# Two transformer blocks on one core: which attention of the first block runs first, and how its steps are spaced

## The chip, the cores and the metric

The kernel runs on one core of a Trainium2 chip. The metric is the device time in microseconds (us) from launch to end, the median of a few executions. TensorE (PE) multiplies matrices, VectorE (DVE) and ScalarE (ACT) work elementwise on SBUF and PSUM, GpSimd (POOL) elementwise on SBUF alone, SyncE (SP) issues transfers.

## The reference

Two transformer blocks follow each other on one sequence of 512 tokens, width 1024, fp32. The change concerns the order of work in the first block, and one spacing that both blocks share. Cut to what matters:

```
def first_block(x, ...):
    proj = rms_norm(x, norm1_g) @ w_in
    qa, ka, va, qb, kb, vb, gate_a, gate_b = split(proj)
    out_a = chunked_attention(qa, ka, va, q_gain, k_gain, rel_bias)  # head norms, bias, softmax
    out_b = stick_breaking_attention(qb, kb, vb)                     # sigmoid, reversed cumulative product
    mixed = sigmoid(gate_a) * (out_a @ w_branch_a) + sigmoid(gate_b) * (out_b @ w_branch_b)
    x = x + mixed @ w_out
    return x + conv_glu(rms_norm(x, norm2_g), ...)

def second_block(x, ...):
    ...  # hgrn2 mixer, and forgetting_attention (head norms, decay, causal softmax)
    merged = gate_h * (y_h @ w_branch_a) + gate_f * (y_f @ w_branch_b)
    ...  # then out projection, gated FFN, and a last gated projection
```

out_a and out_b don't depend on each other.

## The kernel before

Every weight matrix is streamed once, in **slots** of 128 x 512 numbers (256 KB). SP loads a slot into one of four raw buffers; ACT rounds it to a high half `w_hi` (L841), GpSimd subtracts to get the low half `w_lo` (L642); PE does twelve matmuls of 512 columns with it, three products for each of four 128-wide tiles (L1514). The halves have eight buffers, so conversions run up to seven slots ahead of PE.

One list, `SCHEDULE`, gives the order of all work; each engine walks it and does its own part of each entry, strictly in that order, waiting on semaphores for the others. `run(names, plan)` writes the slots of the phases in `names`, numbered from 0 across them; an entry of `plan` with number n stands behind slot n. A phase of one group has eight slots (`branch` phases have two groups of four, `gate` phases two of eight). Behind the last slot of a group stands a `take`: its four PSUM tiles are read out, by ACT or DVE as `OWNER` says (a = ACT, d = DVE), then a `fill` (the conversion of a later slot), and then the plan's entries of that number. PE starts the next group in the same banks, tile by tile as each is taken. In the first block the numbers are: qA 0 to 7, kA 8 to 15, vA 16 to 23, qB 24 to 31, kB 32 to 39, vB 40 to 47, gateA 48 to 63, branchA 64 to 71, gateB 72 to 87, and branchB in a list of its own. In the second: hi, hg, fq, fk, fv 0 to 39, gateH 40 to 55, branchH 56 to 63, gateF 64 to 79.

An attention (A and B in the first block, F in the second) is 16 steps, one per pair of heads and block of 128 queries, and three more to drain; step i handles (i mod 4 + 1) x 128 keys. On PE (`att_pe`) a step does its scores into banks 4 and 5 (L1438), at steps 6, 10, 14 and 18 the product with v for a finished pair (L1453), and the transposes of the probabilities of step i - 2 (L1465). Between lie chains on other engines:

- A: DVE adds the bias and finds the maximum (L1106), ACT takes exp (L757), DVE the reciprocal (L1138), ACT scales (L773); a finished pair is copied by ACT (L766) and its low half formed by DVE (L1144).
- F: as A, with three DVE instructions for bias and maximum (L1116 to L1120), and part of the transposed probabilities copied by ACT (L760).
- B: DVE masks (L1100), ACT takes two sigmoids per head (L748, L749), DVE scans (L1133), GpSimd multiplies (L694).

Head norms (`square`, `scale`) of q and k come ahead of A and F: ACT squares, PE averages (L1612), ACT takes Ln and Exp (L956, L958), DVE scales.

ACT keeps one table of functions; `uses(name)` loads another where the next entry needs it (L848). Exp and Ln are in one, sigmoid is in another, copies work with any. The takes of gateA, gateB, gateH and gateF are sigmoids (L926), those of branchA and branchH DVE multiplies (L1063).

`attention(kind, first, last)` spreads the steps between two slot numbers, in proportion to `room`:

```
room = [min(i, STEPS - 1) % TB + 5 for i in range(STEPS + LAG + 1)]
return [(first + sum(room[:i]) * (last - first + 1) // sum(room), ("att", kind, i)) ...]
```

which places A after slots 24 to 51, B after 53 to 83 and F after 48 to 78; F's steps 5, 6, 7, 13, 14 and 15 stand after 55, 57, 59, 68, 70 and 72.

SP also issues 17 small loads (gains, convolution rows, `rel_bias`), five after each of slots 4 to 7, and after vA's loads the bias table: it waits for `rb_ext`, writes it out, and loads `bias_mask` (2 MB).

Of the kernel before, what the change touches and what calls it, by code (L numbers as in the profile page):

```python
# [17 lines left out]
F32R = mybir.dt.float32r  # L18
U32 = mybir.dt.uint32
ALU = mybir.AluOpType  # L20
ACT = mybir.ActivationFunctionType
AX = mybir.AxisListType

P = 128
S = 512
TB = S // P
# [20 lines left out]
class Phase:  # L47
# [4 lines left out]


PHASES = [Phase(*a) for a in (
    ("qA", 8, 1), ("kA", 8, 1), ("vA", 8, 1), ("qB", 8, 1), ("kB", 8, 1), ("vB", 8, 1),
    ("gateA", 8, 2), ("branchA", 4, 2), ("gateB", 8, 2), ("branchB", 4, 2), ("out1", 8, 2),
    ("up1", 8, 11), ("down1", 22, 2),
    ("hf", 8, 1), ("hq", 8, 1), ("hi", 8, 1), ("hg", 8, 1), ("fq", 8, 1), ("fk", 8, 1), ("fv", 8, 1),
    ("gateH", 8, 2), ("branchH", 4, 2), ("gateF", 8, 2), ("branchF", 4, 2), ("out2", 8, 2),
# [3 lines left out]
for _p in PHASES:  # L63
# [5 lines left out]

OWNER = {name: "adad" for name in ("qB", "kB", "vB", "qA", "kA", "vA", "hi", "fq", "fk", "fv")}  # L70
OWNER |= {name: "aaaa" for name in ("gateB", "gateA", "gateH", "gateF", "pgate", "hq", "hf", "hg")}
OWNER |= {name: "dddd" for name in ("branchA", "branchB", "branchH", "branchF", "out1", "out2",
                                    "down1", "down2", "up1")}
OWNER["up2"] = "aadd"
OWNER["pproj"] = "adad"
# [34 lines left out]
def make_schedule():  # L110
# [25 lines left out]

    def attention(kind, first, last):

        room = [min(i, STEPS - 1) % TB + 5 for i in range(STEPS + LAG + 1)]
        return [(first + sum(room[:i]) * (last - first + 1) // sum(room), ("att", kind, i))  # L140
                for i in range(len(room))]

# [6 lines left out]
    def residual(name, norm, plan=(), meanwhile=None):  # L149
# [12 lines left out]
        if meanwhile:  # L162
# [6 lines left out]
    s.append(("start",))  # L169
    s.extend([("sumsq", 0, 0), ("vec", 0), ("warm", 0), ("norm", 0, 0), ("prefill", 4), ("prefill", 5),  # L170
              ("norm", 0, 1), ("prefill", 6), ("prefill", 7)])
    run(["qA", "kA", "vA", "qB", "kB", "vB", "gateA", "branchA", "gateB"],
        [(8, ("vec", 1))] + head_norms("qA", "kA", 9, 17) + attention("A", 24, 52) + attention("B", 53, 85))
    run(["branchB"])
    residual("out1", 1)
    s.append(("up", "up1"))
    residual("down1", 2, [(4, ("foxw",))])
# [125 lines left out]
def two_block_kernel(nc, a, out):  # L303
    ctx = ExitStack()
    with ctx:
# [47 lines left out]
        def u(name, kb, shape, dt=F32):  # L353
            return place(name, shape, dt, offset=U + kb * KB)
# [8 lines left out]
        rb = u("rb", 58, [NH, NREL])  # L363
        rb_ext = u("rb_ext", 60, [NH, 640])

        qk1 = {"qA": u("qA", 0, [P, 4, S]), "kA": u("kA", 8, [P, 4, S]), "qB": u("qB", 24, [P, 4, S]),
               "kB": u("kB", 32, [P, 4, S]), "fq": u("fq", 72, [P, 4, S]), "fk": u("fk", 80, [P, 4, S])}
        vtok = {"vA": u("vA", 16, [P, 4, S]), "vB": u("vB", 40, [P, 4, S]),
                "fv": u("fv", 88, [P, 4, S]), "hi": u("hv", 24, [P, 4, S])}

        bias_mask = u("bias_mask", 48, [P, NH, S])
        yA = (u("yA_hi", 64, [P, 4, S], F32R), u("yA_lo", 72, [P, 4, S], F32R))
        yB = (u("yB_hi", 80, [P, 4, S], F32R), u("yB_lo", 88, [P, 4, S], F32R))
        keep = [u(f"keep{i}", 48 + 2 * i, [P, S]) for i in range(2)]
        after = [u(f"after{i}", 52 + 2 * i, [P, S]) for i in range(2)]
        sig_halves = {"gateA": (0, 8), "gateB": (64, 72), "gateH": (56, 64), "gateF": (48, 16), "pgate": (16, 24)}
        sig = {name: [u(f"{name}{i}", kb, [P, 4, S]) for i, kb in enumerate(v)] for name, v in sig_halves.items()}

        probs_t = {}
        for kind, kb in (("A", 88), ("B", 16), ("F", 40)):  # L380

            apart, skip = (104 - kb) // 2, (96 - kb) // 2
            both = u(f"probs_t{kind}", 112 - 4 * apart, [P, 2, apart, S])
            probs_t[kind] = both[:, :, skip:skip + TB, :]
# [76 lines left out]
        def gate(name, j):  # L461

            return sig[name][j // 4][:, j % 4, :]
# [91 lines left out]
        def _(e):  # L555
# [42 lines left out]
            for i, p in enumerate(PHASES):  # L598
                if p.name in ("up1", "up2"):
                    with e.Fori(0, p.groups) as g:  # L600
                        for k in range(p.kc):
                            load(p.name, g, k, g * p.kc + (p.slot0 + k))
                else:
                    for g in range(p.groups):
                        for k in range(p.kc):
                            load(p.name, g, k, p.slot0 + g * p.kc + k)
                            if p.name == "qA" and k >= RAW_SLOTS:
                                for _ in range(5):
                                    next(small, None)
                if p.name == "vA":  # L610


                    e.wait_ge(rb_ready, 1)
                    e.dma_start(bias_dram, rb_ext[:, :]).then_inc(scratch_full, 16)
                    e.wait_ge(scratch_full, 16)
                    e.dma_start(bias_mask[:, :, :], bass.AP(bias_dram.tensor, 0, [[1, P], [640, NH], [1, S]])).then_inc(bias_full, 16)
                if p.name == "up2":

                    h_done(e, 3, DC - 2)
                    h_done(e, 3, DC - 1)  # L620
                    e.dma_start(ptok[:, :, :], a["p_2"][0, 0].rearrange("(t p) c -> p t c", p=P)).then_inc(p_full, 16)
# [204 lines left out]
        def _(e):  # L826
# [43 lines left out]
            for x in SCHEDULE:  # L870
# [38 lines left out]
                elif what == "take":  # L909
# [5 lines left out]
                    for n in range(first, end):  # L915
# [16 lines left out]
                        elif name == "pproj":  # L932
                            link(e.activation(pproj[:, 4 * g + n, :], bank, ACT.Copy))
                            e.nop().then_inc(taken["a"], 1)
                            if first_bank(name, g) == 4:
                                e.nop().then_inc(bank_free[4 + n], 1)
                    if name in ("branchB", "branchF"):
                        for n in range(4):
                            j = 4 * g + n
                            e.wait_ge(mix_ready, (DC if name == "branchF" else 0) + j + 1)  # L940
                            e.activation(h_hi[:, j, :], gate("gateB" if name == "branchB" else "gateF", j), ACT.Copy).then_inc(mixhi_ready, 1)
                elif what == "square":
                    tile_taken(e, x[1], 0, x[2])
                    square(qk1[x[1]][:, x[2], :])
                elif what == "scale":
# [84 lines left out]
        def take_dve(e, name, g, first, end, link):  # L1030
# [11 lines left out]
            for n in range(first, end):  # L1042
                if OWNER[name][n] != "d":
                    continue
                tile_ready(e, name, g, n)
                j = 4 * g + n
                bank = ps[first_bank(name, g) + n][:, :]
                if name in ("qB", "kB", "qA", "kA", "fq", "fk"):
                    o, i_ = in_query_order(name, n, bank)
                    e.tensor_scalar(o, i_, HD ** -0.5 if name == "qB" else 1.0, None,  # L1050
                                    ALU.mult).then_inc(taken["d"], 1)
                elif name in vtok:
                    e.tensor_copy(vtok[name][:, n, :], ps[n][:, :]).then_inc(taken["d"], 1)
                elif name == "pproj":
                    link(e.tensor_copy(pproj[:, j, :], bank))
                    e.nop().then_inc(taken["d"], 1)
                    if first_bank(name, g) == 4:
                        e.nop().then_inc(bank_free[4 + n], 1)
                elif name in ("branchA", "branchH"):

                    t = gate("gate" + name[-1], j)
                    tile_taken(e, "gate" + name[-1], g, n)
                    e.tensor_tensor(t, ps[n][:, :], t, ALU.mult).then_inc(taken["d"], 1)  # L1063
                elif name in ("branchB", "branchF"):
                    first, second = ("gateA", "gateB") if name == "branchB" else ("gateH", "gateF")
                    t = gate(second, j)
                    tile_taken(e, second, g, n)
                    e.tensor_tensor(t, ps[n][:, :], t, ALU.mult).then_inc(taken["d"], 1)
                    e.wait_ge(taken["d"], taken_before(name, g, "d") + n + 1)
                    e.tensor_tensor(t, t, gate(first, j), ALU.add).then_inc(mix_ready, 1)  # L1070
                elif name in ("out1", "out2", "down1", "down2"):
                    k = {"out1": 1, "down1": 2, "out2": 3, "down2": 4}[name]
                    e.tensor_tensor(xT[:, j, :], bank, xT[:, j, :], ALU.add).then_inc(x_ready, 1)  # L1073
                    e.wait_ge(x_ready, k * DC + j + 1)
                    e.nop().then_inc(taken["d"], 1)
                    if first_bank(name, g) == 4:
                        e.nop().then_inc(bank_free[4 + n], 1)
            if name in ("branchB", "branchF"):
                for n in range(4):
                    j = 4 * g + n  # L1080
                    e.wait_ge(mixhi_ready, (DC if name == "branchF" else 0) + j + 1)
                    e.tensor_tensor(h_lo[:, j, :], gate("gateB" if name == "branchB" else "gateF", j),
                                    h_hi[:, j, :].bitcast(F32), ALU.subtract).then_inc(mixlo_ready, 1)

        def att_dve(e, kind, i, link):
# [383 lines left out]
        def _(e):  # L1469
# [15 lines left out]
            def activations_ready(name, g, k):  # L1485

                first = isinstance(g, int) and g == 0
                if not first:
                    return
                if name in norm_of and name in ("qA", "up1", "hf", "up2", "pgate"):  # L1490
                    h_done(e, norm_of[name], k)
                elif name in ("out1", "out2"):
                    e.wait_ge(mixlo_ready, (DC if name == "out2" else 0) + k + 1)
# [227 lines left out]
```

## Time and profile before

| | us |
|---|---|
| median of three executions | 1656.02 |
| lowest, highest | 1655.26, 1656.29 |
| the profiled execution, its own time | 1656.29 |
| its span, first to last instruction | 1654.5 |
| PE busy, share of the span | 98% |
| DVE, ACT, POOL busy | 34%, 42%, 47% |
| granted clock of PE, mean | 0.997 |

Read the busy shares with care: matmuls overlap, so PE's records touch even where its pace is slower than it could be. A time in a row of the timeline is from the span's start. The row of an instruction after an idle time names what ended it.

### The profile page before, as it was taken

Reading aid. Unit: us, or ns where it says so; the run is one execution under the profiler, and the core shown is the slowest. Engines: PE = TensorE matmul, PEld = TensorE weight load, DVE = VectorE, ACT = ScalarE, POOL = GpSimd, SP = SyncE. Lnnn points to the kernel's source line nnn. Section 1 sums busy time; section 2 is a strip of 40 time slices with the busy share of each in tenths; the row PEclk is TensorE's granted clock in tenths of the full one; section 3 lists DMA queues with packets and bytes.
Section 4 is the critical chain, followed back from the end, with each engine's and each line's share of the span. In section 5 each row is a group of like instructions: output and inputs, shape, how many; then the busy total and the mean of one; then the engine's idle time right before and its main releaser. Section 6 shows DMA issues by size and latency. Waiting matters only on the chain.

```text
span 1654.5 us, 21926 instructions
## 1 busy us (share of the span) xinstructions
PE 1624.3 (98%) x7416; PEld 1282.9 (78%) x7416; DVE 560.5 (34%) x911; ACT 691.8 (42%) x1223; POOL 773.3 (47%) x605
## 2 busy tenths in 40 slices
PE   8999999999999999999999999999999999999998
PEld 6777777777888888887788777767778888888877
DVE  4134346343433333013565333551541111100044
ACT  5465454433544444223533444654343333322242
POOL 7432366543644444543765323233445444444442
PEclk9999999999999999999999999999999999999999
DMA  4522221222333333322322213221214333323212
GB/s 145 158 72 63 74 73 58 77 86 67 105 100 91 92 95 102 109 96 57 110 71 64 71 52 127 65 70 65 89 50 129 97 98 93 112 96 97 95 63 83
DMA packets 103203, 145.52 MB, mean 88 GB/s; under 512 B 11093, under 2 KB 56894, under 8 KB 102990
## 3 DMA queue, kind: packets, MB, share of 16 engines
q1 hardware_dynamic: 102958, 142.30, 28.9%
q10 hardware_dynamic: 160, 2.11, 0.4%
q8 instruction: 50, 0.82, 0.2%
q14 instruction: 35, 0.29, 0.1%
HBM read 142.24 MB, written 2.13 MB: 87 GB/s over the span
## 4 chain that ended last, share of the span: by engine, by line
PE 90%; DVE 4%; ACT 3%; POOL 2%; issue 1%; DMA 1%; DVEq 0%; ACTq 0%; SPq 0%
PE bank L1514 79%; PE bank L1438 2%; PE bank L1465 2%; PE bank L1453 2%; DVE work L1352 2%; PE bank L1639 2%; POOL w_lo L642 1%; PE bank L1612 1%; ACT L848 1%; POOL h_lo L491 1%; DMA w_raw<-in_w_in 1%; ACT h_hi L908 0%; DVE h_lo L491 0%; PE bank L1660 0%; PE bank L1674 0%
## 5 line engine op out<-in xcount | busy, mean ns | idle before, releaser
L642 POOL TENSOR_TENSOR w_lo<-w_raw,w_hi 128x512 fp32r<-128x512 f32 x516 | 680.7, 1328 | 733.2 <-ACT w_hi L841 732.1
L841 ACT ACTIVATE w_hi<-w_raw 128x512 fp32r<-128x512 f32 x516 | 317.6, 628 | 642.8 <-PE bank L1514 561.0
L1514 PE MATMUL bank<-h_hi,w_lo 128*128 128x512 f32 x1376 | 546.9, 397 | 11.9 <-ACT gateF L926 4.8
L1514 PE MATMUL bank<-h_hi,w_hi 128*128 128x512 f32 x1376 | 537.1, 390 | 0.0
L1514 PE MATMUL bank<-h_lo,w_hi 128*128 128x512 f32 x1376 | 536.6, 390 | 0.0
L1514 PEld LDWEIGHTS bank<-h_hi,w_lo 128*128 128x128 f32 x1376 | 258.9, 188 | 74.7 <-issue 8.8
L1514 PEld LDWEIGHTS bank<-h_hi,w_hi 128*128 128x128 f32 x1376 | 258.8, 188 | 54.8
L1514 PEld LDWEIGHTS bank<-h_lo,w_hi 128*128 128x128 f32 x1376 | 259.1, 188 | 54.0 <-issue 2.2
L1514 PE MATMUL bank<-g_hi,w_lo 128*128 128x512 f32 x352 | 137.0, 389 | 0.0
L1514 PE MATMUL bank<-g_hi,w_hi 128*128 128x512 f32 x352 | 136.9, 389 | 0.0
L1514 PE MATMUL bank<-g_lo,w_hi 128*128 128x512 f32 x352 | 136.9, 389 | 0.0
L1162 DVE SCALAR_TENSOR_TENSOR acc<-bank,vec,acc 128x511 f32<-128x511 f32 x88 | 62.9, 746 | 144.8 <-ACT acc L796 139.7
L1073 DVE TENSOR_TENSOR xT<-bank,xT 128x512 f32<-128x512 f32 x32 | 22.1, 691 | 224.9 <-PE bank L1514 222.6
L1173 DVE TENSOR_TENSOR acc<-bank,acc 128x512 f32<-128x512 f32 x22 | 15.2, 691 | 199.6 <-ACT acc L807 196.5
L1514 PE MATMUL bank<-w_lo,h_hi 128*128 128x512 f32 x192 | 80.1, 417 | 2.8 <-POOL w_lo L642 2.4
L1514 PEld LDWEIGHTS bank<-g_hi,w_lo 128*128 128x128 f32 x352 | 66.1, 188 | 13.8
L1514 PEld LDWEIGHTS bank<-g_hi,w_hi 128*128 128x128 f32 x352 | 66.1, 188 | 13.8
L1514 PEld LDWEIGHTS bank<-g_lo,w_hi 128*128 128x128 f32 x352 | 66.1, 188 | 13.6
L1514 PE MATMUL bank<-w_hi,h_hi 128*128 128x512 f32 x192 | 75.8, 395 | 0.0
L1514 PE MATMUL bank<-w_hi,h_lo 128*128 128x512 f32 x192 | 75.6, 394 | 0.0
L491 POOL TENSOR_TENSOR h_lo<-work,h_hi 128x512 fp32r<-128x512 f32 x20 | 29.2, 1458 | 81.4 <-ACT h_hi L908 81.4
L757 ACT ACTIVATE work<-work,mneg 128x128 f32<-128x128 f32 (+3 forms) x64 | 36.0, 563 | 65.5 <-DVE mneg L1120 40.0
(262 smaller groups left out, 1619.9 us busy)
## 6 DMA issues: line engine op xcount, KB each, us to landing
w_raw<-in_w_in SPq DMA_DIRECT2D x168, 256.0 KB
w_raw<-in_w_ffn_up SPq DMA_DIRECT2D x88, 256.0 KB
w_raw<-in_w_ffn_down SPq DMA_DIRECT2D x88, 256.0 KB
w_raw<-in_w_ffn_gate SPq DMA_DIRECT2D x88, 128.0 KB
w_raw<-in_w_ffn_up SPq DMA_DIRECT2D x88, 128.0 KB
w_raw<-in_w_out SPq DMA_DIRECT2D x32, 256.0 KB
w_raw<-in_w_branch_a SPq DMA_DIRECT2D x16, 256.0 KB
w_raw<-in_w_branch_b SPq DMA_DIRECT2D x16, 256.0 KB
```

The costliest lines, as they stand in the source:

```text
L491: e.tensor_tensor(h_lo[:, j, :], work[j % 2][:, :], h_hi[:, j, :].bitcast(F32), ALU.subtract).then_inc(hlo_ready[j % 2], 1)
L642: e.tensor_tensor(w_lo[:, pos % SPLIT_SLOTS, :], w_raw[:, pos % RAW_SLOTS, :], w_hi[:, pos % SPLIT_SLOTS, :].bitcast(F32), ALU.subtract).t ...
L757: e.activation(ring, ring, ACT.Exp, scale=-1.0 if kind == "A" else 1.0, bias=mneg[:, k, j:j + 1], accum_out=rsum[:, k, j:j + 1]).then_inc( ...
L841: e.activation(w_hi[:, pos % SPLIT_SLOTS, :], w_raw[:, r, :], ACT.Copy).then_inc(hi_full, 1)
L1073: e.tensor_tensor(xT[:, j, :], bank, xT[:, j, :], ALU.add).then_inc(x_ready, 1)
L1162: e.scalar_tensor_tensor(out=o, in0=ps[banks + n][:, 0:S - shift], scalar=vec[:, conv_col(tap, col, n // 2)], in1=o, op0=ALU.mult, op1=ALU ...
L1352: e.scalar_tensor_tensor(out=work[j % 2][:, :], in0=xT[:, j, :], scalar=vec[:, gain + j:gain + j + 1], in1=work[2][:, :], op0=ALU.mult, op ...
L1438: e.matmul(banks[h][:, 0:n], qk1[qn][r, pair, qb * P:n], qk1[kn][r, pair, 0:n], start=True, stop=True).then_inc(a_["sc_done"], 1)
L1453: mm = e.matmul(bank[64 * h:64 * h + 64, c * P:S], vtok[vn][:, c, d], probs_t[kind][:, h, c, c * P:S], start=c == 0, stop=c == TB - 1, ski ...
L1465: mm = e.transpose(bank[:, o:o + P], work[(2 * j + h) % 4][:, c * P:(c + 1) * P], ident[:, :])
L1514: mm = e.matmul(ps[banks + n][:, :], l, r, start=k == 0 and i == 0, stop=k == p.kc - 1 and i == 2)
L1639: mm = e.matmul(of_level(lev, bank[:, c]), k_[:, h, c], of_level(lev, q_[:, h, c]), start=True, stop=True)
```

## The change

The first block does B's projections and attention first and A's second; gateB and branchB come before gateA and branchA. Buffers are exchanged to match: B's q, k, v are where A's were, `keep` and `after` lie in what later holds yA. Head norms of A stand behind B's attention, and the first of them waits until B's last product with v is done, since buffers overlap. The first steps of B stand after slot 19, those of A after 59. In `room` 5 becomes 3, for A, B and F, so narrow steps get less of the spacing and wide ones more; F keeps its first and last slot numbers. The small loads are issued one per slot from slot 4 on, the bias table after slot 31's load, and the vectors and `rb_ext` are prepared after slot 16 in place of slot 8.

```diff
-    ("qA", 8, 1), ("kA", 8, 1), ("vA", 8, 1), ("qB", 8, 1), ("kB", 8, 1), ("vB", 8, 1),
-    ("gateA", 8, 2), ("branchA", 4, 2), ("gateB", 8, 2), ("branchB", 4, 2), ("out1", 8, 2),
+    ("qB", 8, 1), ("kB", 8, 1), ("vB", 8, 1), ("qA", 8, 1), ("kA", 8, 1), ("vA", 8, 1),
+    ("gateB", 8, 2), ("branchB", 4, 2), ("gateA", 8, 2), ("branchA", 4, 2), ("out1", 8, 2),
...
-        room = [min(i, STEPS - 1) % TB + 5 for i in range(STEPS + LAG + 1)]
+        room = [min(i, STEPS - 1) % TB + 3 for i in range(STEPS + LAG + 1)]
...
-    run(["qA", "kA", "vA", "qB", "kB", "vB", "gateA", "branchA", "gateB"],
-        [(8, ("vec", 1))] + head_norms("qA", "kA", 9, 17) + attention("A", 24, 52) + attention("B", 53, 85))
-    run(["branchB"])
+    run(["qB", "kB", "vB", "qA", "kA", "vA", "gateB", "branchB", "gateA"],
+        [(16, ("vec", 1))] + attention("B", 19, 47) + head_norms("qA", "kA", 49, 53) + attention("A", 59, 85))
+    run(["branchA"])
...
-        yA = (u("yA_hi", 64, [P, 4, S], F32R), u("yA_lo", 72, [P, 4, S], F32R))
-        yB = (u("yB_hi", 80, [P, 4, S], F32R), u("yB_lo", 88, [P, 4, S], F32R))
-        keep = [u(f"keep{i}", 48 + 2 * i, [P, S]) for i in range(2)]
-        after = [u(f"after{i}", 52 + 2 * i, [P, S]) for i in range(2)]
+        yB = (u("yB_hi", 64, [P, 4, S], F32R), u("yB_lo", 72, [P, 4, S], F32R))
+        yA = (u("yA_hi", 80, [P, 4, S], F32R), u("yA_lo", 88, [P, 4, S], F32R))
+        keep = [u(f"keep{i}", 80 + 2 * i, [P, S]) for i in range(2)]
+        after = [u(f"after{i}", 84 + 2 * i, [P, S]) for i in range(2)]
...
-                            if p.name == "qA" and k >= RAW_SLOTS:
-                                for _ in range(5):
-                                    next(small, None)
-                if p.name == "vA":
+                            if p.name == "kB" or p.name == "vB" or (p.name == "qB" and k >= RAW_SLOTS):
+                                next(small, None)
+                if p.name == "qA":
...
                 elif what == "square":
+                    if x[1:] == ("qA", 0):
+                        e.wait_ge(A["B"]["pv_done"], PAIRS)
                     tile_taken(e, x[1], 0, x[2])
...
-                elif name in ("branchA", "branchH"):
+                elif name in ("branchB", "branchH"):
...
-                elif name in ("branchB", "branchF"):
-                    first, second = ("gateA", "gateB") if name == "branchB" else ("gateH", "gateF")
+                elif name in ("branchA", "branchF"):
+                    first, second = ("gateB", "gateA") if name == "branchA" else ("gateH", "gateF")
```

The other lines exchange the same names.

## Rows read from the trace of the kernel before

**Rows 1.** The page's first part: busy us, share of the span, instructions.
```profile
PE 1624.3 (98%) x7416; PEld 1282.9 (78%) x7416; DVE 560.5 (34%) x911; ACT 691.8 (42%) x1223; POOL 773.3 (47%) x605
```
**Rows 2.** Waits of PE: for whom, us in total, times, longest.
```profile
PE bank L1514 <- ACT gateF L926: 4.8, 1, 4.8
...
PE bank L1514 <- ACT hk L931: 2.8, 1, 2.8
PE bank L1514 <- POOL w_lo L642: 2.4, 1, 2.4
PE bank L1514 <- ACT qA L922: 1.6, 1, 1.6
...
PE bank L1514 <- ACT gateA L926: 0.5, 1, 0.5
PE bank L1453 <- ACT probs_tF L760: 0.4, 1, 0.4
```
**Rows 3.** The chain of waits, in up1 and down1: start, us, what, instructions.
```profile
411.88 359.37 PE bank L1514 x1584
```
**Rows 4.** Timeline of PE: start, us, engine, line, operation, tiles, shape, count.
```profile
98.78 0.50 PE L1514 MATMUL bank<-h_hi,w_lo 128*128 128x512 f32 x1
...
180.23 0.48 PE L1514 MATMUL bank<-w_lo,h_hi 128*128 128x512 f32 x1
...
184.64 0.47 PE L1514 MATMUL bank<-w_lo,h_hi 128*128 128x512 f32 x1
...
210.72 0.49 PE L1438 MATMUL bank<-kB,qB 64*128 64x128 f32 x4
...
225.85 0.47 PE L1514 MATMUL bank<-h_hi,w_lo 128*128 128x512 f32 x1
...
1112.09 0.48 PE L1514 MATMUL bank<-h_hi,w_lo 128*128 128x512 f32 x1
...
1114.70 0.39 PE L1514 MATMUL bank<-h_hi,w_hi 128*128 128x512 f32 x1
1119.86 0.77 PE L1514 MATMUL bank<-h_hi,w_lo 128*128 128x512 f32 x1 [4.77 <-ACT gateF L926]
...
1126.73 0.48 PE L1514 MATMUL bank<-h_hi,w_lo 128*128 128x512 f32 x1
```
**Rows 5.** Timeline of ACT, the same columns.
```profile
187.84 1.34 ACT L773 ACTIVATE work<-work,rinv 128x512 f32<-128x512 f32 x2 [0.23 <-DVE rinv L1138]
...
211.54 1.28 ACT L848 ACT_TABLE_LOAD   x1
...
213.57 0.27 ACT L749 ACTIVATE work<-bank 128x128 f32<-128x128 f32 x1
...
227.89 0.59 ACT L749 ACTIVATE work<-bank 128x512 f32<-128x512 f32 x1
...
1116.70 1.11 ACT L773 ACTIVATE work<-work,rinv 128x384 f32<-128x384 f32 x2
...
1119.12 2.06 ACT L926 ACTIVATE gateF<-bank 128x512 f32<-128x512 f32 x4
```
**Rows 6.** Timeline of DVE, the same columns.
```profile
100.14 0.08 DVE L1106 DVE_READ_ACCUMULATOR2_ANT mneg<- 128x1 f32 x1
...
183.34 0.69 DVE L1144 TENSOR_TENSOR yA_lo<-bank,yA_hi 128x512 fp32r<-128x512 f32 x1 [0.32 <-ACT yA_hi L766]
...
228.17 1.22 DVE L1133 TENSOR_TENSOR_SCAN after<-keep 128x511 f32<-128x511 f32 x1
...
1131.63 0.17 DVE L1138 RECIPROCAL rinv<-rsum 128x2 f32<-128x2 f32 x1 [0.28 <-ACT work L757]
```
**Rows 7.** Busy time by stretch: from:to, us, PE busy, granted clock, DMA share, GB/s.
```profile
800.00:806.00 6.00, 3.68 (x16) 1.00 0.65 175
...
1120.00:1126.00 6.00, 6.00 (x16) 0.56 0.15 46
...
1606.00:1612.00 6.00, 5.76 (x18) 0.72 0.56 165
```

More of the change, by code:

```diff
@@ L71 @@
 OWNER |= {name: "aaaa" for name in ("gateB", "gateA", "gateH", "gateF", "pgate", "hq", "hf", "hg")}
-OWNER |= {name: "dddd" for name in ("branchA", "branchB", "branchH", "branchF", "out1", "out2",
+OWNER |= {name: "dddd" for name in ("branchB", "branchA", "branchH", "branchF", "out1", "out2",
                                     "down1", "down2", "up1")}
@@ L364, in two_block_kernel @@
         rb_ext = u("rb_ext", 60, [NH, 640])
-        qk1 = {"qA": u("qA", 0, [P, 4, S]), "kA": u("kA", 8, [P, 4, S]), "qB": u("qB", 24, [P, 4, S]),
-               "kB": u("kB", 32, [P, 4, S]), "fq": u("fq", 72, [P, 4, S]), "fk": u("fk", 80, [P, 4, S])}
-        vtok = {"vA": u("vA", 16, [P, 4, S]), "vB": u("vB", 40, [P, 4, S]),
+        qk1 = {"qB": u("qB", 0, [P, 4, S]), "kB": u("kB", 8, [P, 4, S]), "qA": u("qA", 24, [P, 4, S]),
+               "kA": u("kA", 32, [P, 4, S]), "fq": u("fq", 72, [P, 4, S]), "fk": u("fk", 80, [P, 4, S])}
+        vtok = {"vB": u("vB", 16, [P, 4, S]), "vA": u("vA", 40, [P, 4, S]),
                 "fv": u("fv", 88, [P, 4, S]), "hi": u("hv", 24, [P, 4, S])}
         bias_mask = u("bias_mask", 48, [P, NH, S])
-        yA = (u("yA_hi", 64, [P, 4, S], F32R), u("yA_lo", 72, [P, 4, S], F32R))
-        yB = (u("yB_hi", 80, [P, 4, S], F32R), u("yB_lo", 88, [P, 4, S], F32R))
-        keep = [u(f"keep{i}", 48 + 2 * i, [P, S]) for i in range(2)]
-        after = [u(f"after{i}", 52 + 2 * i, [P, S]) for i in range(2)]
-        sig_halves = {"gateA": (0, 8), "gateB": (64, 72), "gateH": (56, 64), "gateF": (48, 16), "pgate": (16, 24)}
+        yB = (u("yB_hi", 64, [P, 4, S], F32R), u("yB_lo", 72, [P, 4, S], F32R))
+        yA = (u("yA_hi", 80, [P, 4, S], F32R), u("yA_lo", 88, [P, 4, S], F32R))
+        keep = [u(f"keep{i}", 80 + 2 * i, [P, S]) for i in range(2)]
+        after = [u(f"after{i}", 84 + 2 * i, [P, S]) for i in range(2)]
+        sig_halves = {"gateB": (0, 8), "gateA": (64, 72), "gateH": (56, 64), "gateF": (48, 16), "pgate": (16, 24)}
         sig = {name: [u(f"{name}{i}", kb, [P, 4, S]) for i, kb in enumerate(v)] for name, v in sig_halves.items()}
         probs_t = {}
-        for kind, kb in (("A", 88), ("B", 16), ("F", 40)):
+        for kind, kb in (("B", 88), ("A", 16), ("F", 40)):
             apart, skip = (104 - kb) // 2, (96 - kb) // 2
@@ L936, in _ @@
                                 e.nop().then_inc(bank_free[4 + n], 1)
-                    if name in ("branchB", "branchF"):
+                    if name in ("branchA", "branchF"):
                         for n in range(4):
@@ L940, in _ @@
                             e.wait_ge(mix_ready, (DC if name == "branchF" else 0) + j + 1)
-                            e.activation(h_hi[:, j, :], gate("gateB" if name == "branchB" else "gateF", j), ACT.Copy).then_inc(mixhi_ready, 1)
+                            e.activation(h_hi[:, j, :], gate("gateA" if name == "branchA" else "gateF", j), ACT.Copy).then_inc(mixhi_ready, 1)
                 elif what == "square":
+                    if x[1:] == ("qA", 0):
+                        e.wait_ge(A["B"]["pv_done"], PAIRS)
                     tile_taken(e, x[1], 0, x[2])
@@ L1077, in take_dve @@
                         e.nop().then_inc(bank_free[4 + n], 1)
-            if name in ("branchB", "branchF"):
+            if name in ("branchA", "branchF"):
                 for n in range(4):
@@ L1081, in take_dve @@
                     e.wait_ge(mixhi_ready, (DC if name == "branchF" else 0) + j + 1)
-                    e.tensor_tensor(h_lo[:, j, :], gate("gateB" if name == "branchB" else "gateF", j),
+                    e.tensor_tensor(h_lo[:, j, :], gate("gateA" if name == "branchA" else "gateF", j),
                                     h_hi[:, j, :].bitcast(F32), ALU.subtract).then_inc(mixlo_ready, 1)
@@ L1489, in activations_ready @@
                     return
-                if name in norm_of and name in ("qA", "up1", "hf", "up2", "pgate"):
+                if name in norm_of and name in ("qB", "up1", "hf", "up2", "pgate"):
                     h_done(e, norm_of[name], k)
```

## The prediction

> **What bounds the kernel now.** The page comes first: TensorE (PE) is busy for 1624.3 of 1654.5 us [rows 1]. Time is added only where PE waits or runs slowly, so the second view is the list of PE's waits [rows 2]. The reader is to see how little there is to win: of what the change touches, the first block's large waits are 1.6 us for tile 0 of qA and 0.5 us for gateA, and the second block's largest is 4.8 us for gateF. The chain of waits gives the pace: 1584 matmuls in 359.37 us are 0.227 us each, 2.72 us for the twelve of a slot [rows 3]. Beside attention a slot costs more: from PE's timeline, slot end to slot end, I take 2.85 us, as slot 71 of the second block shows (first matmul at 1112.09, the last at 1114.70, and 0.23 for it: 2.84) [rows 4].
>
> The third view is the timeline of the three engines about the one long wait, which is the pattern for everything below. Step 14 of attention F is placed after slot 70, the take of gateF after slot 71. PE leaves step 14 at 1112.09 and ends slot 71 at 1114.93. ScalarE (ACT) obeys the same order: it scales step 14's probabilities until 1117.81 (1116.70 + 1.11), loads the sigmoid table, and starts the four sigmoids at 1119.12; PE goes on at 1119.86 [rows 4, 5]. So a take of ACT waits for the whole chain of the step ahead of it, and then for the table.
>
> **How to place things.** A take comes after the last slot of a group and ahead of a step with the same number; that step then gives PE about 1 to 3 us of work before it needs the taken bank. Working the formula of the changed kernel: B steps 0 to 18 stand after slots 19, 19, 21, 22, 24, 25, 27, 28, 30, 31, 32, 34, 36, 37, 38, 40, 42, 44, 46; A after 59, 59, 61, 62, 64, 65, 66, 68, 69, 70, 71, 73, 75, 76, 77, 78, 80, 82, 84; F after 48, 49, 50, 52, 54, 55, 56, 58, 60, 61, 63, 65, 67, 68, 69, 71, 73, 75, 77. ACT takes gateB after 55 and 63, gateA after 79 and 87; VectorE (DVE) takes branchB after 67 and 71; the second block has ACT's takes after 55, 71 and 79, DVE's after 59 and 63.
>
> **What is removed.** In the first block the 0.5 us at gateA [rows 2] goes, with short ones of the same kind that I put at 0.4: -0.9. The 1.6 us for qA at the start stays: ACT's takes wait for conversions of weights that land late, paced by GpSimd's first conversions; the small transfers sit ahead of them but the weight loads wait for GpSimd anyway. I cost their spreading at nothing, bounds -1.6 and +1. The 2 MB bias table moves from ahead of slot 24's load to ahead of slot 32's; seven converted slots, 20 us of PE, cover it as before: 0, with a rival below.
>
> **New waits in the first block**, each as (end of the chain ahead) less (end of PE's work), from the end of PE's step:
> - After 19, steps 0 and 1 of B together. Step 1's scores need step 0's banks. Before, PE was through with step 0 at about 211.2 (210.72 + 0.49); ACT's table load (211.54) and sigmoids ended at 213.57 + 0.27, so +2.7 for the second bank, and step 1 then takes PE 0.3 more, against 0.6 undisturbed: +2.4 [rows 4, 5].
> - After 22, step 3 of B (512 wide), take of vB after 23. ACT is done at 227.89 + 0.59, +2.6, DVE's scan at 228.17 + 1.22, +3.5, from 225.85; a tile's copy is 0.7, and PE wants tile 1 at 2.85 + 0.68: +0.7 [rows 4 to 6].
> - After 38, step 14, take of kA after 39: the pattern of the 0.5 us at gateA [rows 2], with a little for DVE: +0.75.
> - Head norms now span a gate's take (55): table in 1.28, four sigmoids 2.06, table back 1.28, then Ln, 0.6 like the sigmoid of 512 columns at 227.89, before the bank of the next mean is free. That is 0.4 + 0.85: +1.25 (below 0: no; above: 2.6, both loads bare).
> - After 59, two steps of A: the second bank is free about 100.14 + 0.08, +1.45 from PE's 98.78, again with 0.3 for the rest and some 0.5 off for the undisturbed part: +1.3 [rows 4, 6].
> - After 62, step 3 of A (512 wide), take of gateB after 63, no step between. ACT's chain ends at 187.84 + 1.34, 4.54 from 184.64 [rows 4, 5]. For F's step 14 it was 5.72 and PE's stop, slot end to slot start, 1119.86 - 1114.93 = 4.93. Same pattern: 4.93 - 1.18 = **+3.75**.
> - After 66, step 6 of A, take of branchB by DVE after 67. DVE ends A's low half at 183.34 + 0.69, 3.8 from 180.23; the link and a multiply of the same size, 0.7, bring 4.7, less 2.85: +1.85 [rows 4, 6]. After 71 step 10 covers: 0.
> - After 78, step 15 (512 wide), take of gateA after 79: as after 62, **+3.75**.
> Sum 15.75. More table loads come with it, but away from these places each (1.28) fits into idle time of ACT, 2 us in most slots: 0. Net for the block 14.9.
>
> **Attention F**, moved by the smaller constant alone. Step 14 is now two slots ahead of gateF's take, and step 15 (1.5 us of PE) is behind it: the tile is there at about 7.7, PE at 7.2. The stop of 4.93 falls to 0.5. After that stop PE ran slowly: the granted clock was 0.56 on average from 1120 to 1126, most of it the 1.2 GHz level, so 6 x (1 - 0.56) = 2.65 were lost [rows 7]. Both go: -7.1. A further 0.4, the wait for ACT's copy of probs_tF where step 10 stands one slot behind step 9 [rows 2], goes too, but comes back twice: step 14 is one slot behind step 13, of the same widths, +0.45; step 6 is one slot behind step 5, whose chain is also held by a table load of 1.28 behind the take, of which I put half on top, +1.15. And step 7 (512 wide) is now directly ahead of DVE's take of branchH (58, 59): its reciprocal ends at 1131.63 + 0.17, 5.07 from 1126.73; a multiply more is 5.8, less 2.85: +2.95 [rows 4, 6]. Net for F: -7.1 - 0.4 + 0.45 + 1.15 + 2.95 = -2.95.
>
> **The clock of the new stops.** Three stops of about 3 to 3.75 us are new. Before, an idle time of 4.8 dropped PE to half clock, one of 2.8 (wait for hk) did not (granted 1.00 from 800 to 806), one of 2.4 behind other waits did (0.72 from 1606 to 1612) [rows 2, 7]. So each new one may or may not; the price is 2.65 as at gateF, or 6 us x (1 - 0.72) = 1.7 as at 1606. I take one of three, 2.2; bounds 0 and 8.
>
> **Sum.** 14.9 - 2.95 + 2.2 = 14.15, rounded to 14. The profiled execution took 1656.29 us, 0.27 above the median of 1656.02, so the forecast is 1670.0 against the median.
>
> **A rule of the skill.** Between the copy that ends at 1117.81 and the first sigmoid at 1119.12 lie 1.31 us: the load of 1.28 and nothing else [rows 5]. The Trainium skill, "ScalarE: Activation LUTs", section "What ACT_TABLE_LOAD costs", puts a switch at 2.66 us, the load of 1.28 and a drain of 1.38. By the rule each of the three bare switches here (55, 63, 79) would stop PE 1.38 longer, 4.1 in all, and the time would be 1674. The trace disagrees on the drain; I keep the row.
>
> **Rivals.**
> - *The clock drops at every new stop* (20 in 100). Price 3 x 2.65 in place of 2.2, +6: 1676. For: an idle time of 2.4 sufficed once. Against: one of 2.8 did not.
> - *A transfer is late* (12 in 100): the bias table now lands while B's steps crowd ACT and GpSimd, and weights of slots 32 on come late by some us. Price as the start's wait and hk's together, 1.6 to 6: 1672 to 1679. Against: about 20 us of cover.
> - *The relief at gateF decides, faster* (8 in 100). One mechanism: PE has enough other work ahead of it to cover the chains of ACT and DVE before each take. Then the two stops of 3.75, DVE's 1.85 and 2.95 and the clock's 2.2 are not there, and 14.15 - 14.5 is -0.35; if the pairs after 19 and 59 are covered as well (3.7) and the start's 1.6 goes, it is -5.7: 1650. It decides from where all new waits sum to less than the 8.4 that they replace (0.9 + 7.1 + 0.4). For: 7.1 us of relief stand in one place. Against: A's 4.54 and F's 5.07 are measured, and one slot is 2.85.
> - *It moves the waits and no more* (8 in 100): half of the sum is absorbed, about 1657 to 1659. Within 0.2%, 3.3 us, no timing of this kernel tells a change.
> - *The skill's drain exists in this place* (2 in 100): 1674.
> The forecast has the remaining 50.
>
> **Numbers.** Likeliest 1670. The range 1659.5 to 1678 leaves out the faster case, most of the absorbed one and the worst clock and transfer cases. Faster by over 0.2% 8, within 9, slower 83 in 100.
>
> **What would show it.** In the changed profile: PE waits of about 3.5 us for gateB once and gateA once in the first block, behind a table load of ScalarE; 1.5 to 2 us for branchB's multiply; about 2.4 us between the first two B steps, on ACT; a wait of 3 us for branchH's multiply; gateF's 4.8 us gone and with it the low clock about 1118. If gateB's and gateA's waits are under 1 us the forecast is wrong by 5 or more; if low clock shows at both, it is short by 3 to 5.

## The result, and the profile after

The changed kernel takes 1685.58 us (median of 4, 1684.88 to 1686.38) against 1656.13 (median of 4) for the kernel before: ratio 1.0174, 95% interval 1.0161 to 1.0186. That is 29.5 us slower, where 14 were forecast; 1685.6 lies outside the range. The direction and the places were right; the size was half. The profiled execution was one of the quicker ones: 1681.14 us, 24.9 above the profiled one of before.

The list of PE's waits in the kernel after; each row answers to one of [rows 2], or to a step of the prediction:

```profile
PE bank L1515 <- ACT gateB L925: 4.0, 2, 3.6
PE bank L1515 <- ACT gateA L925: 3.6, 1, 3.6
PE bank L1515 <- ACT hk L930: 2.9, 1, 2.9
PE bank L1515 <- DVE gateH L1064: 2.8, 1, 2.8
PE bank L1439 <- ACTq L750: 2.8, 1, 2.8
PE bank L1515 <- POOL w_lo L641: 2.4, 1, 2.4
PE bank L1515 <- DVE gateB L1064: 2.0, 1, 2.0
PE bank L1613 <- ACTq L958: 1.7, 2, 0.9
PE bank L1515 <- ACT qB L921: 1.7, 1, 1.7
PE bank L1439 <- DVEq L1110: 1.6, 1, 1.6
...
PE bank L1454 <- ACT probs_tF L759: 1.4, 2, 1.0
...
PE bank L1515 <- ACT gateF L925: 0.9, 1, 0.9
PE bank L1515 <- ACT kA L921: 0.5, 1, 0.5
PE bank L1515 <- ACT vB L923: 0.5, 1, 0.5
```

The reader is to see the two stops of 3.6 at the takes of gateB and gateA, 2.8 between the first two steps of B (bank of L1439 held by ACT), 1.6 between those of A, 2.0 at branchB's multiply (it waits under the name gateB, L1064), and 2.8 at branchH's. gateF's 4.8 is down to 0.9. Start and hk are as they were.

PE's waits in the whole list, those at the start included, sum to 41.1 us, against 25.7 in the kernel before: 15.4 more.

The chain of waits of the kernel after, about slot 63 (start, us, what):

```profile
250.86 0.69 DVE work L1107
...
252.79 1.33 ACT work L772 x2
254.15 1.28 ACT L847
255.44 0.61 ACT gateB L925
256.05 0.14 issue
256.18 4.58 PE bank L1515 x12
```

Step 3 of A left PE at 249.59; its scaled probabilities are done at 254.12, 4.53 later, then the table, then the first sigmoid, then PE. This is the pattern that [rows 5] showed at gateF. And the last row is new: twelve matmuls took 4.58 us where a slot takes 2.76 beside attention. The cause is in the granted clock. Busy time by stretch, kernel after (from:to, us, PE busy, granted clock, DMA share, GB/s):

```profile
79.00:87.00 8.00, 6.83 (x19) 0.57 0.62 198
257.00:261.00 4.00, 4.00 (x14) 0.57 0.13 25
277.00:281.00 4.00, 3.60 (x9) 0.57 0.23 68
332.00:339.00 7.00, 5.42 (x14) 0.51 0.09 30
827.00:831.00 4.00, 3.40 (x9) 0.57 0.67 189
1092.00:1102.00 10.00, 7.18 (x38) 1.00 0.25 60
```

0.57 and 0.51 mean that most of the stretch was at the 1.2 GHz level. Behind the first B pair, gateB, branchB, gateA and hk PE was slow; behind branchH it was not. PE's busy time in a stretch, times (1 - clock), estimates what the low clock cost there: 2.9, 1.7, 1.5, 2.7 and 1.5 us, in the order of the rows, 10.3 in all. For the profile before the same estimate gave 2.65 behind gateF.

### The profile page after: what moved, and what is told of

The parts are those of the page before. It is cut to its first block, busy times and chain, and to the rows that moved or that the text cites. A ratio compares the mean times of both kernels' runs of the same rounds, so it can differ in the third digit from the quotient of the medians.

```text
span 1679.4 us, 21935 instructions
## 1 busy us (share of the span) xinstructions
PE 1633.4 (97%) x7416; PEld 1287.4 (77%) x7416; DVE 560.0 (33%) x911; ACT 701.7 (42%) x1231; POOL 772.8 (46%) x605
## 4 chain that ended last, share of the span: by engine, by line
PE 88%; DVE 4%; ACT 4%; issue 1%; POOL 1%; DMA 1%; DVEq 0%; ACTq 0%; SPq 0%
PE bank L1515 78%; PE bank L1439 2%; PE bank L1466 2%; PE bank L1454 2%; DVE work L1353 1%; PE bank L1640 1%; ACT L847 1%; PE bank L1613 1%; POOL w_lo L641 1%; POOL h_lo L491 1%; ACT h_hi L907 0%; DVE h_lo L491 0%; PE bank L1661 0%; DMA w_raw<-in_w_in 0%; PE bank L1675 0%
## 5 line engine op out<-in xcount | busy, mean ns | idle before, releaser
L1174 DVE TENSOR_TENSOR acc<-bank,acc 128x512 f32<-128x512 f32 x22 | 15.2, 692 | 199.7 <-ACT acc L806 196.5
```

## The experiments

Every run was timed against the kernel before on its own chip (medians 1656.26 to 1656.84 there).

**The old constant with the exchange.** `room` gets 5 again.

```diff
-        room = [min(i, STEPS - 1) % TB + 3 for i in range(STEPS + LAG + 1)]
+        room = [min(i, STEPS - 1) % TB + 5 for i in range(STEPS + LAG + 1)]
```

> The changed kernel with the old constant 5 in room, for A, B and F; the exchange of A and B stays. B's steps then stand after 19, 20, 21, 23, ..., 37, 39; A's after 59, 60, 61, 62, ..., 77, 79; F's as before. Placement theory: gone are the stop between the first two B steps (3.0 and 2.45 of slow clock), the waits for vB and kA (1.0, 1.1), the one between the first two A steps (1.65) and the stop at gateA's take (3.65 and 2.4): -15.3; gateF's stop comes back, +3 net: about 1673, with steps 3 and 6 of A still stopping PE at gateB and branchB. Rival, the exchange itself (order of projections, loads, tables) costs the 25 us: 1680 or more.

Measured: 1667.29 us, ratio 1.0062 (1.0045 to 1.0079). 18 of the 29 us went with one digit, 6 more than expected. The exchange cannot be the cause of these 18. PE's waits sum to 32.3 us here, 8.8 less than in the kernel after. The rest goes with the clock: the mean granted clock of its four runs is 0.9950, of the changed kernel's thirteen 0.990, and 0.005 of 1667 us is 8.

**F alone.** The kernel before, with 3 in `room` for F.

```diff
-        room = [min(i, STEPS - 1) % TB + 5 for i in range(STEPS + LAG + 1)]
+        room = [min(i, STEPS - 1) % TB + (3 if kind == 'F' else 5) for i in range(STEPS + LAG + 1)]
```

> The kernel before with 3 in room for attention F alone. Prediction's step for F: -3 (the stop at gateF and its slow clock go, waits at step 6, step 14, gateF's take and branchH's multiply come): 1653. Rival: the new stop of 3 us at branchH drops the clock as others do in the changed kernel: 1654.5 to 1656, no change.

Measured: 1656.34, ratio 0.9997 (0.9987 to 1.0007): no change, as the rival said. Its waits and two stretches:

```profile
PE bank L1514 <- DVE gateH L1063: 2.8, 1, 2.8
PE bank L1514 <- ACT hk L931: 2.7, 1, 2.7
...
PE bank L1453 <- ACT probs_tF L760: 1.4, 2, 1.0
```

```profile
802.00:808.00 6.00, 5.03 (x12) 0.53 0.62 165
1075.00:1079.00 4.00, 4.00 (x12) 0.57 0.19 48
```

gateF's stop of 4.8 is down to 0.9, branchH's 2.8 is there, and here the clock fell behind it (1075 to 1079), 1.7 lost, and behind hk's 2.7 as well, which the change does not touch. The same stop of 2.8 left the clock alone in the kernel after.

**Idle matmuls in the stops.** Nothing is moved; PE multiplies the identity by a constant, result unread, in four of the stops. `BUSY` gives for each slot number the bank and how many matmuls stand behind it; the lines that place them in the list are left out here.

```diff
+BUSY = {19: (7, 3), 63: (5, 4), 67: (5, 2), 79: (5, 4)}
...
+                elif what == "busy":
+                    bank = bank_wait(e, x)
+                    for i in range(BUSY[x[1]][1]):
+                        mm = e.matmul(bank[:, :], ident[:, :], chunk_start[:, :], start=True, stop=True)
+                    mm.then_inc(bank_free[BUSY[x[1]][0]], 1)
```

> The changed kernel with idle matmuls (identity by a constant, 0.9 us each, result unread) in four stops: 3 between the first two steps of B, 4 behind slot 63, 2 behind 67, 4 behind 79. They do no work and only keep PE busy. Clock theory: the waits stay, the slow stretches behind them go: profile of after lost 2.45 + 1.7 + 1.7 + 2.4 = 8.3 there, so about 8 to 11 us faster than the changed kernel: 1675 to 1678. Rival, the slow stretches have no part or the matmuls come too late: 1685 or more.

Measured: 1674.42, ratio to before 1.0106 (1.0090 to 1.0123), 11.2 below the changed kernel with thirteen matmuls more. PE's timeline between the first two B steps, and stretches about the four places, of this kernel (the second and the last row are two other stops, the first A pair and branchH):

```profile
77.13 0.49 PE L1449 MATMUL bank<-kB,qB 64*128 64x128 f32 x4
77.56 2.84 PE L1568 MATMUL bank<-chunk_start,ident 128*128 128x512 f32 x6
80.44 0.70 PE L1449 MATMUL bank<-kB,qB 64*128 64x256 f32 x4
```

```profile
76.00:84.00 8.00, 7.96 (x33) 1.00 0.35 95
...
235.00:241.00 6.00, 5.74 (x19) 0.72 0.12 44
...
245.00:260.00 15.00, 14.86 (x64) 1.00 0.16 41
266.00:285.00 19.00, 18.76 (x91) 1.00 0.18 52
320.00:345.00 25.00, 24.86 (x111) 1.00 0.19 58
...
1092.00:1098.00 6.00, 5.19 (x18) 0.72 0.16 44
```

Step 1 starts as late as before (3.31 after step 0, in both), but the clock is 1.00 in all four. So some 11 us of the 29 in the timed runs are slow clock: the mean clock of the four runs is 0.9968 against 0.990, and 0.0067 of 1680 us is 11 as well. The waits themselves are most of the rest. The profiled execution, 1676.10, is only 5.0 below the profiled one of after: in it the clock fell behind the first A pair (0.72) and behind branchH (0.72), where it had held in the kernel after. 11 is thus the net of four stops kept at full clock and of what the clock did at the others.

**Steps away from the takes.** Exchange and F as changed; B and A placed by hand.

```diff
+        at = {"B": [19, 20, 21, 23, 24, 25, 27, 28, 30, 31, 32, 34, 36, 37, 39, 40, 42, 44, 46],
+              "A": [59, 60, 61, 63, 65, 66, 67, 69, 70, 71, 72, 74, 75, 76, 77, 79, 81, 83, 85]}
+        if kind in at:
+            return [(n, ("att", kind, i)) for i, n in enumerate(at[kind])]
```

> The changed kernel with the steps of B and A placed by hand so that no wide step stands one slot ahead of a take without a step behind it, and no two steps share a slot; exchange and F (constant 3) as changed. Placement theory: all of the first block's new stops but the head norms' (1.9) go, with their clock: -24 in the profile and more in the timed runs: 1656 to 1660. Rival, the exchange itself: above 1665.

Measured: 1658.38, ratio 1.0013 (1.0004 to 1.0023). 27 of the 29 us are in the placement of A's and B's steps. The waits left in the first block (the head norms' row and gateB's), and the one at the start, qB's:

```profile
PE bank L1618 <- ACTq L963: 1.7, 2, 0.9
PE bank L1520 <- ACT qB L926: 1.7, 1, 1.7
...
PE bank L1520 <- ACT gateB L930: 0.4, 1, 0.4
```

One of the two 0.9 and the 0.4 belong to the head norms that span gateB's take, 1.3 in all; the stops at the takes of gateB, gateA and branchB are gone.

**Two steps moved by one slot.** In the changed kernel, A's step 3 from 62 to 63, step 15 from 78 to 79.

```diff
+        at = {'A': [59, 59, 61, 63, 64, 65, 66, 68, 69, 70, 71, 73, 75, 76, 77, 79, 80, 82, 84]}
```

> The changed kernel with two steps moved by one slot: A's step 3 from behind 62 to behind 63, step 15 from behind 78 to behind 79, so that the gate's take stands ahead of them. Placement theory: the two stops of 3.65 go, with the slow clock behind them (1.7 + 2.4 in the profile, perhaps 2 x 2.65 in the timed runs): 11 to 13 less than 1685.6, 1673 to 1675. Rival, the steps' chains are only moved and PE waits elsewhere in A: above 1680.

Measured: 1670.37, ratio to before 1.0077 (1.0061 to 1.0092): 15.2 below the changed kernel, half of the whole loss, by two numbers. Two waits of 3.6 are 7.2 of it. That leaves 8 for the clock, more than the profile of after had shown behind them (about 4.4); the mean clock of its four runs, 0.9955 against 0.990, gives 9.

**No table at the gates of the first block.** The takes of gateB and gateA copy; the sigmoid of both gates is left out.

```diff
-                            e.activation(gate(name, 4 * g + n), bank, ACT.Sigmoid).then_inc(taken["a"], 1)
+                            f = ACT.Copy if name in ("gateB", "gateA") else ACT.Sigmoid
+                            e.activation(gate(name, 4 * g + n), bank, f).then_inc(taken["a"], 1)
```

> The changed kernel without the sigmoid of gateB and gateA: their takes are copies, so that ACT loads no table for them (this part of the computation is left out). If a switch costs the load alone (1.28), the waits at the takes behind 63 and 79 fall from 3.6 to 2.4 and the 1.9 us at 55 go: -4.5 and up to -5 of clock, 1676 to 1681. If a switch costs 2.66, with a drain, the two waits fall to 1.0: -7.5 and the clock, 1673 to 1677. The waits of PE in the profile tell the two apart.

Measured: 1673.99, 11.6 below the changed kernel. By the median alone this lies in the range expected with a drain and 2 us below the one expected for the load alone. The two ranges differ by the waits, though, and the waits and ACT's timeline decide for the load alone:

```profile
PE bank L1516 <- ACT gateA L926: 2.1, 1, 2.1
PE bank L1516 <- ACT gateB L926: 2.1, 1, 2.1
```

```profile
250.64 1.33 ACT L772 ACTIVATE work<-work,rinv 128x512 f32<-128x512 f32 x2 [0.23 <-DVE rinv L1140]
251.88 2.04 ACT L926 ACTIVATE gateB<-bank 128x512 f32<-128x512 f32 x4
```

The two waits fell from 3.6 to 2.1: 1.5 each, where the load alone says 1.28 and a drain on top 2.66. Some of the 0.2 is overlap: without a load the take starts 0.09 before the scaling ahead of it ends. The further fall of the median is clock: the four runs have a mean of 0.994 against 0.990, some 6.7 us. It also shows that most of the stop, 2.1 of 3.6, is the chain and not the table.

**Pairs apart.** Step 1 of B behind slot 20, of A behind 60.

```diff
+        at = {'A': [59, 60, 61, 62, 64, 65, 66, 68, 69, 70, 71, 73, 75, 76, 77, 78, 80, 82, 84], 'B': [19, 20, 21, 22, 24, 25, 27, 28, 30, 31, 32, 34, 36, 37, 38, 40, 42, 44, 46]}
```

> The changed kernel with the second step of B behind slot 20 and the second of A behind 60, in place of 19 and 59. The waits between the paired steps go: 2.9 + 2.45 of slow clock behind it, and 1.65: 7 less, 1678 to 1679. Rival, ACT's table load ahead of B's first step stops PE wherever step 1 stands: 1683 or more.

Measured: 1675.75, ratio to before 1.0109 (1.0093 to 1.0124): 9.8 less than the changed kernel, where 7 were expected. The waits between the paired steps (2.8 and 1.6) are not in its list any more; the mean clock, 0.9938 against 0.990, accounts for about 6 more. The load ahead of B's first step makes no wait once a slot stands between the steps.

**The constant alone in the first block.** The kernel before, A first, 3 in `room` for A and B, 5 for F.

```diff
-        room = [min(i, STEPS - 1) % TB + 5 for i in range(STEPS + LAG + 1)]
+        room = [min(i, STEPS - 1) % TB + (5 if kind == 'F' else 3) for i in range(STEPS + LAG + 1)]
```

> The kernel before, A first as it was, with 3 in room for A and B and 5 for F: the constant alone in the first block. By the placement rule: A's steps 0 and 1 share slot 24 (+1.65), step 5 stands one slot ahead of the take of qB behind 31 (ACT's chain 4.0 and a copy 0.6, less 2.85: +1.8), B's step 11 one slot ahead of branchA's take behind 71 (DVE 3.5 + 0.7 - 2.85: +1.4), 0.3 at step 11 of A goes: +4.5, 1660.8. No table load is at any of them. Rival, only stops behind gates with a table load count: 1656 to 1657.

Measured: 1662.68 against 1656.82, ratio 1.0039 (1.0025 to 1.0053), 5.9 slower. The three stops forecast are these rows of its waits: qB's, the first A pair's, and branchA's multiply, which waits under the name gateA:

```profile
PE bank L1514 <- ACT qB L922: 1.6, 1, 1.6
PE bank L1438 <- DVEq L1109: 1.6, 1, 1.6
...
PE bank L1514 <- DVE gateA L1063: 1.3, 1, 1.3
```

Forecast were 1.8, 1.65 and 1.4. They sum to 4.5; behind the pair's 1.6 the clock fell too (granted 0.72 from 100 to 106), which the forecast of 4.5 had left out. The rule of placement carries over to the other order, and to takes without a table.

**F by hand, both orders.** Two lists for F in the kernel before, the first also in the exchanged one placed by hand.

```diff
+        at = {'F': [48, 49, 50, 51, 53, 55, 57, 59, 61, 62, 63, 64, 65, 66, 68, 71, 73, 75, 77]}
...
+        at = {'F': [48, 49, 50, 51, 53, 55, 57, 59, 61, 62, 63, 64, 66, 67, 68, 71, 73, 75, 77]}
```

> The kernel before with F's steps by hand: after 48, 49, 50, 51, 53, 55, 57, 59, 61, 62, 63, 64, 65, 66, 68, 71, 73, 75, 77, so that each gate's take has two slots or a step between itself and the chain ahead. Placement theory: gateF's 4.8 and its 2.65 of slow clock and gateH's 1.3 go, about 0.4 comes at one-slot distances behind wide steps: 8 to 9 less than before, 1647.5 to 1648.5. Rival, the saved waits come back at later steps as in the run of F alone: 1653 or more.

> The exchanged order with B, A and F all placed by hand (the lists of the run away from takes, and F's of the kernel before by hand). If only placement matters, F's list takes 9 us off 1658.4, to about 1649.5, and it stays 1 to 2 us above the kernel before with F by hand, by the head norms that span gateB's take (1.9). Rival, the exchange has a gain of its own: 1647 or less.

> The kernel before with F by hand, second list: step 12 behind slot 66 in place of 65, 13 behind 67 in place of 66, the rest as in the first list. In the first, step 12 waited 1.4 for DVE one slot behind a wide step, and the clock was low behind it (1.7). Both should go, 0.4 for ACT's copy comes: 2 to 2.5 less than 1651.0, about 1648.5. Rival, the median is set by clock losses elsewhere (hk, pgate) and moves under 1 us.

Measured: first list 1650.98, ratio 0.9970 (0.9960 to 0.9980); the exchanged order with it 1652.21, 0.9975 (0.9965 to 0.9984); second list 1649.39, **0.9958 (0.9945 to 0.9972)**, the lowest median here. The first list missed its number by 3: step 12, one slot behind the 512-wide step 11 and after DVE's take of branchH, waited 1.4 for DVE, and the clock fell behind it (granted 0.72 from 1094 to 1100). The exchanged order missed by 2.7: the same wait of 1.4 is in its list, but there the clock stayed at 1.00. Its other two rows are the head norms that span gateB's take; the kernel before waits 0.9 once at head norms. The wait in the first list, then the three rows of the exchanged order:

```profile
PE bank L1441 <- DVEq L1122: 1.4, 1, 1.4
```

```profile
PE bank L1621 <- ACTq L966: 1.7, 2, 0.9
...
PE bank L1447 <- DVEq L1128: 1.4, 1, 1.4
...
PE bank L1523 <- ACT gateB L933: 0.4, 1, 0.4
```

The second list has no such wait of step 12. Its three longest waits behind the first 15 us are far from any attention; short ones remain (0.9 at head norms, 0.5 at gateA, 0.7 for probs_tF). It was to gain 2 to 2.5 on the first list and its median is 1.6 lower, but the two ratios' intervals overlap: what the row shows, the time does not by itself.

```profile
PE bank L1517 <- ACT hk L934: 2.8, 1, 2.8
PE bank L1517 <- POOL w_lo L645: 2.4, 1, 2.4
PE bank L1517 <- ACT qA L925: 1.6, 1, 1.6
```

With F's first list in both, the two orders differ by 1.2 us, and the intervals of their ratios overlap. The exchange has no gain that these runs show. It has a small loss in the list of waits, the 1.3 at the head norms; the medians agree in sign (1.2 here, 2.1 in the run with A and B by hand, where F's constant alone had cost nothing), but the time alone doesn't resolve it.

## Why the prediction was right in kind and wrong in size

**Waits of the first block: right.** Forecast and list side by side: first B pair 2.4, measured 2.8; vB 0.7 and kA 0.75, 0.5 each; head norms 1.25, 1.3 (0.9 of L958's two, and 0.4 of gateB's 4.0); first A pair 1.3, 1.6; gateB 3.75, 3.6; branchB 1.85, 2.0; gateA 3.75, 3.6. Forecast sum 15.75, measured 15.9. No single one is off by more than 0.4, though that the sum is off by only 0.15 is partly luck: the pairs came out 0.7 longer, the others 0.55 shorter. Each could be read from the kernel before, as end of the chain ahead less PE's work.

**Waits of F: right, its clock not.** branchH's 2.95 came as 2.8, the copies' 1.6 as 1.4, gateF fell to 0.9 where I had 0.5. Net of the waits: forecast -0.3, measured -4.8 + 0.9 + 2.8 + (1.4 - 0.4) = -0.1. But the -2.95 of the prediction rests on the 2.65 of slow clock that go with gateF's stop, and the run of F alone, 0 and not -3, shows low clock behind branchH's stop in its place. There too the step was the clock: this new stop had a third of one drop in the prediction, and the relief at gateF was counted in full.

**The clock of the new stops: this step failed.** The prediction says "Three stops of about 3 to 3.75 us are new" and takes "one of three, 2.2". It left out the stops that it had itself forecast at 2.4 (first B pair, measured 2.8) and 1.85 (branchB, 2.0), though its own row of an idle time of 2.4 that dropped the clock spoke for them; the clock fell behind both. And it took one in three where the profile after has low clock behind four of the five stops, and behind hk's too, which the change only shifts in time. The term was 2.2 less 2.65, -0.45; in the profile after it is 2.9 + 1.7 + 1.5 + 2.7 + 1.5 less 2.65, about 7.7. With 15.4 of waits that makes 23.1 of the 24.9 us between the two profiled executions. In the timed runs it is larger: of the thirteen executions those at 1681 had mean clocks of 0.991 to 0.993, those at 1685 to 1687 0.988 to 0.990, and 0.003 of 1684 us is 5 us. The idle matmuls put a measured number on it: 11.2 us with the waits in place. The sum for the timed kernel is then about 15.4 (waits) + 11 to 12 (clock, from 0.990 against 0.997 for the kernel before), and some 2 to 3 that the list does not show; slower restarts behind each new stop may be that part, which was not measured by itself. The prediction's own sign, low clock at both gates, did show; it had priced it at 3 to 5 us short, and the forecast was 15.6 short.

**The rivals.** "The clock drops at every new stop" came nearest: the clock fell at four of five new stops, not at every one, and the rival was priced at three, 1676. The late transfer did not come: the list after has no wait for one behind the start. The relief at gateF was real (4.8 to 0.9) and did not decide. The drain did not show: beside the 1.31 us between ACT's last scaling and the sigmoid in the kernel before stands now 1.5 us of wait saved for a load taken away. So the 2.66 that the Trainium skill, "ScalarE: Activation LUTs", section "What ACT_TABLE_LOAD costs", gives for a switch is not paid here.

**What I said of the start** (1.6 us stays, small transfers cost nothing): right, 1.7 for qB after.

## What to carry to other kernels

Where engines walk one list in order, what an entry costs is set by its neighbours: before an entry that frees a bank, count the slots since the last long chain on the same engine, and leave as much PE work as the chain is long, or put the step behind it. Price an idle time of PE of 2 us or more twice, once as the wait and once as the slow clock behind it (1.5 to 2.9 us here), and give the second a chance nearer three in four than one in three; one of 1.4 to 1.6 us is not safe either (the counts are below). A spacing constant that helps one stop and makes five is judged by the list of distances, not by its intent.

## What the runs showed of the hardware

- In the thirteen profiles here, before, after and eleven runs, low clock stood behind 38 of the 51 stops of PE of 2.0 us or more (those of the first 60 us left out), behind 4 of the 8 of 1.4 to 1.6 us, and behind none of the shorter ones. One of 1.6 us (first A pair) did it in three runs and not in the kernel after; one of 3.4 (hk, in F's first list) did not. branchH's 2.8 did in five of seven profiles, hk's stop, the same work in every kernel, in nine of thirteen. The same stop has no fixed price.
- The kernel before spreads over 1654.2 to 1658.0 in all its runs here, the changed one over 1681.1 to 1687.3; the slower executions have the lower mean clock.
- A load of ScalarE's table, at the end of a chain that PE waits for, costs the 1.28 us of its row and about 0.1 to 0.2 more. Away from such places it made no wait: the changed kernel with A and B by hand has 30 loads where the kernel before has 22, and its only new waits in the first block are the 1.3 us at the head norms.
